# Bidirectional RWKV recurrence in a two-block kernel: running sums in two buffers, the next chunk's exponentials and keys begun mid-step, the first keys ahead of the rows, another order at the end of a step on VectorE

## The chip, the cores and the metric

The kernel runs on one core of a Trainium2 chip. The metric is device time in microseconds, the median of several runs. TensorE (PE in the profile), VectorE (DVE), ScalarE (ACT), GpSimd (POOL) and the queue of SyncE (SP) each run their own list of instructions in order and meet only through semaphores.

## The reference, cut to what matters

Two transformer blocks in fp32 follow each other. The first one mixes the tokens with a short convolution and a recurrence of RWKV type in two directions, the second one with a chunked linear recurrence and sliding window attention; each ends in a feed-forward layer. The change touches only the recurrence of the first block:

```python
def step(S, inp):                       # per token, 8 heads of 64x64 state
    r_t, w_t, kk_t, b_t, v_t, k_t = inp
    sa = einsum("bhvk,bhk->bhv", S, kk_t)
    S = S * w_t - sa[..., None] * b_t + v_t[..., None] * k_t
    return S, einsum("bhvk,bhk->bhv", S, r_t)
# decay w = exp(-DECAY_SCALE * sigmoid(...)); b = kk * a; k_d = k * (1 + (a - 1) * k_a)
# 256 context tokens, then 512 tokens of x, once forward and once in reverse; y is the sum of both
```

## The kernel before, in words

The kernel is one program of about 35,000 instructions. Most of its time goes into large fp32 products with 128x512 operands (`split_product`, L677). In between, from about 251 to 541 us of the span, stands the recurrence.

The recurrence works on chunks of L = 64 tokens: 12 chunks (NC), the first 4 (NCC) of the context and 8 (NCX) of x, in both directions d = 0 and 1, all 8 heads at once. Within a chunk the token-by-token recursion is replaced by a triangular system whose inverse is built by doubling over levels 2 to 6. The work is a software pipeline. Every engine runs `for n in range(-2, NC)`, and one step n does three things: it ends chunk n (state in, updates, results), inverts the system of chunk m = n + 1, and prepares chunk q = n + 2 (decays, keys, score products). The order within a step is written out by hand in each engine's list:

- VectorE (L2322): `running_sums(q)` (the scan over the gates, L2244) right behind the first `w_out`; then `x_out` and `x_turned` (L2257, L2264) for levels 2 to 5, `w_out` (L2250), `state_out` (L2300, L2302), the sum for `mod` (L2347). At the end of the step stand `scores_out` (L2293, one for each direction), `w_out` level 6, `first_level` (L2280), `first_turned` (L2287) and `y_last` (L2271).
- ScalarE (L1618): `update_in`, `update_out`, `state_padded`, then `decay_exps(q)` (L1587 to L1591, which exponentiates the running sums and overwrites them with the inverse decays), the copy of `ada_row2` (L1632), `tok_out` (L1597), `keys_in(q + 1)` (8 small operations, L1610), and in steps 4 to 7 `first_result` (L1603), which empties the bank of the results.
- GpSimd (L1961): the decayed rows `kt`, `rt` (L1947, 128x256), the decayed keys `bh`, `kh` (L1947, 64x256, four for each direction) and `undecayed(q + 1)` (L1956, L1957).
- TensorE (L994): `state_in`, `nx` and `dx` (both go through `tiles`, L810), `updates`, a part of another product (`ada_parts`, L623), `state_terms` (L928), `turned` (L894, which reads the key buffer `bk` and so frees it), `results` (L943, L946), and late in the step `scores(q, 0)`, `dx` level 5, `scores(q, 1)` (L883, L885), `nx` and `dx` level 6.

`scores(q, d)` waits for the keys and rows of chunk q (`kt`, `rt`, `bh`, `kh`), for the masks of the chunk before (`nk`), and (L875) for `y_out` of step n: the results bank must be empty. There is one buffer for the running sums per direction (`cum`), one `bk`, and three each of `ktrt` and `plast`.

Ahead of the loop, TensorE and VectorE turn the values (`values_turned`, `values_out`, L2218) and then form a bonus term (`bonus_sum`, `bonus_out`, L2223); GpSimd waits for all of both before it forms the first rows and keys.

Of the kernel before, what the change touches and what calls it, by code (L numbers as in the profile page):

```python
# [171 lines left out]
def two_blocks(nc, xT, ctxT, vec, con, band, w8, w11, lora, gup, outT):  # L172
    with ExitStack() as ctx:
# [144 lines left out]
        gup_sb = Area(NARENA - 4 * P).take(4 * P)  # L318
# [7 lines left out]
        class Scan:  # L326
# [9 lines left out]
            def rest(self, d):  # L336

                A = AS if d else AV
                self.ktrt = A.take(3, NJ, 2 * L)
                self.nk = A.take(2, 2, NJ, 2 * L)  # L340
                self.cum = rstd[:, NJ * L * d:NJ * L * d + NJ * L].rearrange("p (j t) -> p j t", j=NJ)
# [5 lines left out]
                self.plast = AS.take(3, NJ)  # L347
# [8 lines left out]
        assert AV.at <= 9 * TT and AS.at <= NARENA - 4 * P  # L356
# [52 lines left out]
        sem("x_in", "ctx_in", "vec_in", "con_in", "con_in2", "lora_in", "ada_in0", "ada_in1", "ada_in2", "slot_in0", "slot_in1")  # L409
# [113 lines left out]
        def _(sp):  # L523
# [57 lines left out]
            sp.dma_start(gup_sb, gup).then_inc(s["lora_in"], 16)  # L581
# [28 lines left out]
        def _(pe):  # L610
# [222 lines left out]
            def values_turned(c):  # L833

                pe.wait_ge(s["pre_out"], NJ + max(c, 0))
                for j in range(NJ):
                    at = (4 + j) * TT + L * c
                    last = nc.tensor.transpose(banks[6 + c % 2][:, P * j:P * j + P], kv_row[:, at:at + 2 * L], ident)
                last.then_inc(s["pre_mm"], 1)

            def bonus_sum(j):
                pe.wait_ge(s["pre_out"], NJ + NC + 1 + j - 1)
                mm(banks[6 + j % 2][:, :], headones, rkr[:, j, :], start=True, stop=True).then_inc(s["pre_mm"], 1)
# [3 lines left out]
            pe.wait_ge(s["lora_in"], 32)  # L847
# [8 lines left out]
            for c in range(-1, NC):  # L856
                values_turned(c)
            pe.wait_ge(s["rkr"], NJ)
            for j in range(NJ):
                bonus_sum(j)  # L860
            pe.wait_ge(s["gate"], 2 * NJ)
# [190 lines left out]
            for j in range(NJ):  # L1052
                mm(banks[j][:, :], headones, y_sum[:, j, :], start=True, stop=True).then_inc(s["y_mean"], 1)
            for j in range(NJ):
                mm(banks[4 + j][:, :], gup_sb[:, j * P:(j + 1) * P], g_lo, start=True,
                   stop=True).then_inc(s["gate_mm"], 1)
# [327 lines left out]
        def _(se):  # L1384
# [194 lines left out]
            def decay_exps(q):  # L1579

                for d, sc in enumerate(scans):
# [4 lines left out]
                    done("S", d, q - 2)  # L1586
                    act_f(sc.pe[:, :, at:at + L], sc.cum, ACT.Exp, scale=-DECAY).then_inc(s[f"pe{d}"], 1)  # L1587
                    act_f(sc.plast[:, q % 3, :], sc.cum[:, :, end], ACT.Exp, scale=-DECAY).then_inc(s[f"pe{d}"], 1)
                for d, sc in enumerate(scans):
                    done("pe", d, 2 * q + 2)  # L1590
                    act_f(sc.cum, sc.cum, ACT.Exp, scale=DECAY).then_inc(s[f"einv{d}"], 1)  # L1591
# [25 lines left out]
            keys_in(0)  # L1617
            for n in range(-2, NC):  # L1618
# [9 lines left out]
                if q < NC:  # L1628
                    decay_exps(q)
# [6 lines left out]
                if q + 1 < NC:  # L1636
                    keys_in(q + 1)
# [288 lines left out]
        def _(pool):  # L1926
# [31 lines left out]

            undecayed(0)
            pool.wait_ge(s["pre_out"], 2 * NJ + NC + 1)  # L1960
            for n in range(-2, NC - 2):  # L1961
                q = n + 2
                for d, sc in enumerate(scans):
                    at = place(d, q)
                    done("pe", d, 2 * q + 1)
                    done("gu_mm", d, 2 * (q - 3) + 1)
                    times(sc.ktrt[:, q % 3, :, 0:L], kk[:, :, at:at + L], sc.pe[:, :, d:d + L], "kt", d)
                if q >= NCC:
                    for d, sc in enumerate(scans):
                        at = place(d, q) - TC  # L1970
                        done("y_mm", d, q - 3 - NCC + 1)
                        times(sc.ktrt[:, q % 3, :, L:2 * L], rT[:, :, at:at + L], sc.pe[:, :, 1 - d:1 - d + L], "rt", d)
# [3 lines left out]
                for d, sc in enumerate(scans):  # L1976
                    done("einv", d, q + 1)
                    done("tok_mm", d, q)
                    for e, r in enumerate(HALVES):
                        done("bh", d if e else 0, 2 * q + (e or 2 * d))  # L1980
                        times(sc.bk[r, :, 1 - e, :], gates[r, d, 1, place(d, q) // L], sc.cum[r], "bh", d)
                done("bh", 1, 2 * q + 2)
                for d, sc in enumerate(scans):
                    for e, r in enumerate(HALVES):
                        done("kh", d if e else 0, 2 * q + (e or 2 * d))
                        times(sc.bk[r, :, e, :], keys_made(d, q)[r], sc.cum[r], "kh", d)
                done("kh", 1, 2 * q + 2)
# [51 lines left out]
        def _(dve):  # L2039
# [173 lines left out]
            def values_out(c):  # L2213
                dve.wait_ge(s["pre_mm"], NJ + c + 2)
# [6 lines left out]
            def bonus_out(j):  # L2221
                dve.wait_ge(s["pre_mm"], NJ + NC + 1 + j + 1)
# [14 lines left out]
            def running_sums(q, d):  # L2237

                done("bh", d, 2 * q)
                done("kh", d, 2 * q)  # L2240
                to, gate = flat(scans[d].cum), flat(gates[:, d, 0, place(d, q) // L])
# [54 lines left out]
            def state_out(n):  # L2296
                for d, sc in enumerate(scans):
# [4 lines left out]
                    V.tensor_tensor(sc.S[:, (n + 1) % 2], sc.S[:, (n + 1) % 2], spread(sc.plast[:, n % 3, :], NJ, HD),  # L2302
# [13 lines left out]
            for d in both:  # L2316
                running_sums(0, d)
            for c in range(-1, NC):
                values_out(c)
            for j in range(NJ):  # L2320
                bonus_out(j)
            for n in range(-2, NC):  # L2322
# [21 lines left out]
                if ada:  # L2344
# [518 lines left out]
```

## Time and profile before

| | |
|---|---|
| median of 3 runs | 1637.73 us (1637.27 to 1646.07) |
| the profiled execution's own time | 1632.01 us |
| its span | 1629.7 us |
| PE busy | 1499.3 us (92%) |
| DVE busy | 904.2 us (55%) |
| ACT busy | 595.8 us (37%) |
| POOL busy | 257.0 us (16%) |
| largest group, L677 hf_hi, w_up | 424.1 us |
| L810 (the small products of the recurrence) | 147.5 us, 4224 instructions |

Busy shares are averages over stages with different limits. In the stage of the large products TensorE waits for almost nothing. In the recurrence, about 18% of the span, the engines take turns, and what a change is worth there is read from the order of events within a step. Times in the views are microseconds from the start of the span.

### The profile page before, as it was taken

Reading aid. Unit: us, or ns where it says so; the run is one execution under the profiler, and the core shown is the slowest. Engines: PE = TensorE matmul, PEld = TensorE weight load, DVE = VectorE, ACT = ScalarE, POOL = GpSimd, SP = SyncE. Lnnn points to the kernel's source line nnn. Section 1 sums busy time; section 2 is a strip of 40 time slices with the busy share of each in tenths; the row PEclk is TensorE's granted clock in tenths of the full one; section 3 lists DMA queues with packets and bytes.
Section 4 is the critical chain, followed back from the end, with each engine's and each line's share of the span. In section 5 each row is a group of like instructions: output and inputs, shape, how many; then the busy total and the mean of one; then the engine's idle time right before and its main releaser. Section 6 shows DMA issues by size and latency. Waiting matters only on the chain.

```text
span 1629.7 us, 35052 instructions
## 1 busy us (share of the span) xinstructions
PE 1499.3 (92%) x14676; PEld 1239.3 (76%) x14676; DVE 904.2 (55%) x1467; ACT 595.8 (37%) x1035; POOL 257.0 (16%) x280
## 2 busy tenths in 40 slices
PE   5899996999998697999999998999879999999997
PEld 3687873888888486887787886878758788888886
DVE  1624215677677527888896224766454655655222
ACT  3422344334442324434433223536544323232221
POOL 0000003455542010111111121000001111111111
PEclk9899997999999899999999998999979999999998
DMA  8242100333300221222223222312003222222221
GB/s 346 78 150 78 52 27 1 107 107 107 94 17 4 79 73 57 86 95 103 84 96 98 97 91 76 109 54 78 27 27 103 78 103 103 81 99 97 100 95 69
DMA packets 38744, 139.64 MB, mean 86 GB/s; under 512 B 3040, under 2 KB 3552, under 8 KB 38112
## 3 DMA queue, kind: packets, MB, share of 16 engines
q1 hardware_dynamic: 38480, 135.76, 24.4%
q8 instruction: 97, 1.59, 0.4%
q10 hardware_dynamic: 144, 2.10, 0.3%
q14 instruction: 23, 0.19, 0.0%
HBM read 135.75 MB, written 2.10 MB: 85 GB/s over the span
## 4 chain that ended last, share of the span: by engine, by line
PE 62%; DVE 14%; ACT 3%; issue 3%; POOL 0%; DVEq 0%; ACTq 0%; POOLq 0%
PE bank L677 46%; PE bank L810 7%; DVE ffn_sb L2510 5%; PE bank L687 2%; DVE arena L2293 1%; DVE w_up L2123 1%; PE bank L623 1%; PE bank L1291 1%; DVE arena L2280 1%; PE bank L883 1%; ACT w_up L1409 1%; PE bank L894 1%; PE bank L928 1%; PE bank L943 1%; ACT arena L1769 1%
## 5 line engine op out<-in xcount | busy, mean ns | idle before, releaser
L677 PE MATMUL bank<-hf_hi,w_up 128*128 128x512 f32 x1376 | 424.1, 389 | 0.0
L677 PEld LDWEIGHTS bank<-hf_hi,w_up 128*128 128x128 f32 x1376 | 258.3, 188 | 53.1
L677 PE MATMUL bank<-hf_lo,w_up 128*128 128x512 f32 x688 | 269.4, 392 | 8.1 <-DVE w_up L2123 8.1
L677 PE MATMUL bank<-act_hi,w_down 128*128 128x512 f32 x704 | 216.7, 389 | 0.0
L1409 ACT ACTIVATE w_up<-ring 128x1024 fp32r<-128x1024 f32 x88 | 93.0, 1058 | 216.2 <-PE bank L677 216.2
L2123 DVE TENSOR_TENSOR w_up<-ring,w_up 128x1024 fp32r<-128x1024 f32 x88 | 108.1, 1229 | 104.4 <-ACT w_up L1409 104.3
L810 PE MATMUL bank<-arena 64*64 64x32 f32 (+1 forms) x4224 | 147.5, 221 | 16.3 <-DVE arena L2250 9.0
L677 PEld LDWEIGHTS bank<-hf_lo,w_up 128*128 128x128 f32 x688 | 129.1, 188 | 40.9 <-DVE w_up L2123 13.4
L810 PEld LDWEIGHTS bank<-arena 64*64 64x64 f32 x4224 | 137.1, 137 | 26.3 <-DVE arena L2250 10.3
L2510 DVE SCALAR_TENSOR_TENSOR ffn_sb<-ffn_sb 128x512 f32<-128x512 f32 x176 | 151.5, 861 | 5.5
L677 PEld LDWEIGHTS bank<-act_hi,w_down 128*128 128x128 f32 x704 | 132.1, 188 | 27.3
L2020 POOL TENSOR_TENSOR act_lo<-ffn_sb,act_hi 128x512 f32 x44 | 72.9, 1656 | 440.4 <-ACT act_hi L1698 426.8
L677 PE MATMUL bank<-act_lo,w_down 128*128 128x512 f32 x352 | 137.0, 389 | 1.4 <-DVE w_down L2129 1.4
L2123 DVE TENSOR_TENSOR w_in<-ring,w_in 128x1024 fp32r<-128x1024 f32 x48 | 58.5, 1223 | 137.9 <-ACT w_in L1409 137.6
L677 PE MATMUL bank<-hx_hi,w_in 128*128 128x512 f32 x384 | 120.7, 396 | 0.0
L1409 ACT ACTIVATE w_in<-ring 128x1024 fp32r<-128x1024 f32 x48 | 50.5, 1055 | 139.2 <-PE bank L677 131.4
L1426 ACT ACTIVATE w_down<-ring 128x1408 fp32r<-128x1408 f32 x32 | 44.2, 1381 | 155.6 <-PE bank L677 155.6
L2129 DVE TENSOR_TENSOR w_down<-ring,w_down 128x1408 fp32r<-128x1408 f32 x32 | 52.1, 1627 | 86.8 <-ACT w_down L1426 86.7
L677 PE MATMUL bank<-h_hi,w_in 128*128 128x512 f32 x320 | 99.9, 394 | 0.0
L677 PEld LDWEIGHTS bank<-hx_hi,w_in 128*128 128x128 f32 x384 | 73.6, 192 | 15.3
L677 PE MATMUL bank<-hx_lo,w_in 128*128 128x512 f32 x192 | 76.5, 399 | 5.4 <-ACT arena L1484 3.6
L677 PEld LDWEIGHTS bank<-act_lo,w_down 128*128 128x128 f32 x352 | 66.1, 188 | 15.6 <-DVE w_down L2129 1.8
(316 smaller groups left out, 2343.2 us busy)
## 6 DMA issues: line engine op xcount, KB each, us to landing
ring<-w SPq DMA_DIRECT2D x76, 1024.0 KB, 4.9
ring<-w SPq DMA_DIRECT2D x32, 704.0 KB, 4.0
ring<-w SPq DMA_DIRECT2D x64, 256.0 KB, 3.0
arena<-w SPq DMA_DIRECT2D x2, 3072.0 KB, 22.8
x<-xT SPq DMA_DIRECT2D x1, 2048.0 KB, 11.8
arena<-w SPq DMA_DIRECT2D x2, 1024.0 KB, 20.2
x<-xT ACTq DMA_DIRECT2D x1, 2048.0 KB, 7.7
outT<-x SPq DMA_DIRECT2D x4, 512.0 KB, 2.7
```

Source lines behind the costliest of these rows:

```text
L623: last = mm(out[32 * q:32 * q + 32, :].rearrange("r (c m) -> r c m", c=2), siluc[:, 2 * q + k, :], w[:, :, 2 * q + k, :], start=k == 0, st ...
L677: ins = mm(out, w[:, a, k, :], of_block(b, k0 + k), start=first and k == 0 and m == 0, stop=last and k == n - 1 and m == 2)
L687: ins = mm(out, w[:, a, k, :], of_block(b, k), start=k == 0 and m == 0, stop=k == KB - 1 and m == 2)
L810: last = mm(out(j, r), lhs(j, r), rhs(j, r), start=True, stop=True)
L883: mm(bank[d][e][r, at], sc.bk[r, j, e, :], sc.ktrt[r, q % 3, j, 0:n], start=True, stop=True)
L894: last = nc.tensor.transpose(bank[d][1][:, P * j:P * j + P], sc.bk[:, j].rearrange("p e t -> p (e t)"), ident)
L1409: act_f(w[:, 0], slot_view(g)[:, at:at + blocks, :], ACT.Copy).then_inc(s["w_hi"], 1)
L1426: act_f(w_down[half][:, 0], slot_view(g, HALF), ACT.Copy).then_inc(s["w_hi"], 1)
L2020: nc.gpsimd.tensor_tensor(act_lo[:, bass.ds(j, 1), :].rearrange("p a t -> p (a t)"), silu[u], act_hi[:, bass.ds(j, 1), :].rearrange("p a t ...
L2123: V.tensor_tensor(w[:, 1], slot_view(SLOT[name] + u)[:, c * KB:c * KB + KB, :], w[:, 0], ALU.subtract).then_inc(s["w_lo"], 1)
L2129: V.tensor_tensor(w[:, 1], slot_view(SLOT[name] + half, HALF), w[:, 0], ALU.subtract).then_inc(s["w_lo"], 1)
L2510: ins = V.scalar_tensor_tensor(to, pad[u][:, n // 3:n // 3 + GRID_H, n % 3:n % 3 + GRID_W], tap_w[u][:, n:n + 1], to, ALU.mult, ALU.add)
```

## The change: what it does

- The running sums get a second buffer (`cum[q % 2]`), and `plast` a fourth.
- VectorE computes `running_sums(q + 1)` behind `x_turned` level 3 and the `mod` sum of step n instead of `running_sums(q)` behind the first `w_out`. ScalarE does `decay_exps(q + 1)` between `tok_out` and `keys_in(q + 1)` instead of `decay_exps(q)` before `ada_row2`.
- GpSimd goes direction by direction: all rows of one, then of the other, then all keys of one, then of the other. For chunk 0 the keys come ahead of the rows, and begin before the values are turned.
- Ahead of the loop, the bonus comes before the values.
- End of a step on VectorE: `x_out`/`x_turned` level 5 for both directions ahead of `scores_out(q, 0)`, then `w_out` level 6, `first_level` and `first_turned` of direction 0, `scores_out(q, 1)`, `y_last`, and `first_level`, `first_turned` of direction 1.
- The weights `gup` land in another place, later, with a semaphore of their own.

```diff
@@ ScalarE
-                    done("S", d, q - 2)
-                    act_f(sc.pe[:, :, at:at + L], sc.cum, ACT.Exp, scale=-DECAY).then_inc(s[f"pe{d}"], 1)
+                    done("S", d, q - 3)
+                    act_f(sc.pe[:, :, at:at + L], sc.cum[q % 2], ACT.Exp, scale=-DECAY).then_inc(s[f"pe{d}"], 1)
...
             keys_in(0)
+            decay_exps(0)
...
-                if q < NC:
-                    decay_exps(q)
...
                 if q + 1 < NC:
+                    decay_exps(q + 1)
                     keys_in(q + 1)
                 if NCC <= n < NCC + NCX // 2:
                     for d in range(2):
                         first_result(n, d)
@@ GpSimd
             undecayed(0)
-            pool.wait_ge(s["pre_out"], 2 * NJ + NC + 1)
+            steps.last()
+            keys_decayed(0, 0)
+            pool.wait_ge(s["pre_out"], 2 * NJ)
+            keys_decayed(0, 1)
+            rows_decayed(0, 1)
+            pool.wait_ge(s["pre_mm"], 2 * NJ + NC + 1)
+            rows_decayed(0, 0)
+            undecayed(1)
+            for q in range(1, NC):
+                for d in range(2):
+                    rows_decayed(q, d)
...
+                for d in range(2):
+                    keys_decayed(q, d)
@@ VectorE
-                done("bh", d, 2 * q)
-                done("kh", d, 2 * q)
+                done("bh", d, 2 * q - 2)
+                done("kh", d, 2 * q - 2)
...
+            for j in range(NJ):
+                bonus_out(j)
             for c in range(-1, NC):
                 values_out(c)
-            for j in range(NJ):
-                bonus_out(j)
...
-                if 0 < q < NC:
-                    for d in both:
-                        running_sums(q, d)
...
+                if q + 1 < NC:
+                    for d in both:
+                        running_sums(q + 1, d)
...
+                if inv:
+                    for d in both:
+                        x_out(m, d, 5)
+                        x_turned(m, d, 5)
                 if prep:
                     scores_out(q, 0)
                 if inv:
                     for d in both:
-                        x_out(m, d, 5)
-                    for d in both:
-                        x_turned(m, d, 5)
+                        w_out(m, d, 6)
                 if prep:
+                    first_level(q, 0)
+                    first_turned(q, 0)
                     scores_out(q, 1)
                 if inv:
                     for d in both:
-                        w_out(m, d, 6)
+                        y_last(m, d)
                 if prep:
-                    for d in both:
-                        first_level(q, d)
-                    for d in both:
-                        first_turned(q, d)
-                if inv:
-                    for d in both:
-                        y_last(m, d)
+                    first_level(q, 1)
+                    first_turned(q, 1)
@@ SyncE and TensorE
-            sp.dma_start(gup_sb, gup).then_inc(s["lora_in"], 16)
...
+            sp.wait_ge(s["bh0"], 2 * NCC)
+            sp.dma_start(gup_sb, gup).then_inc(s["gup_in"], 16)
```

## Rows read from the trace of the kernel before

**Rows 1.** Timeline before the loop: start, us, engine, line, operation, count, [idle before <-releaser]

```profile
251.72 1.28 DVE L2244 TENSOR_TENSOR_SCAN rstd<-k_,arena 128x256 f32<-128x256 f32 x2 [11.56 <-ACT arena L1547]
...
253.02 2.21 DVE L2218 COPY arena<-bank 64x256 f32<-64x256 f32 x5
...
257.61 6.64 DVE L2218 COPY x<-bank 64x256 f32<-64x256 f32 x15 [0.32 <-PE bank L838]
...
267.85 0.69 DVE L2223 TENSOR_TENSOR arena<-bank,arena 128x512 f32<-128x512 f32 x1 [0.17 <-PE bank L843]
268.62 1.32 POOL L1947 TENSOR_TENSOR arena<-arena 128x256 f32<-128x256 f32 x2 [11.91 <-DVE arena L2223]
270.07 6.36 POOL L1947 TENSOR_TENSOR arena<-arena,rstd 64x256 f32<-64x256 f32 x8
...
274.98 0.37 PE L883 MATMUL bank<-arena 64*64 64x64 f32 x2 [7.17 <-POOL arena L1947]
...
276.18 0.76 DVE L2293 TENSOR_TENSOR arena<-bank,k_ 128x256 f32<-128x256 f32 x2 [7.63 <-PE bank L885]
...
278.44 2.12 DVE L2280 COPY_PREDICATED arena<-k_,arena 64x128 f32<-64x128 uint32 x4
...
282.21 0.29 DVE L2250 TENSOR_TENSOR arena<-bank,k_ 128x128 f32<-128x128 f32 x1 [0.84 <-PE bank L810]
283.06 0.29 DVE L2250 TENSOR_TENSOR arena<-bank,k_ 128x128 f32<-128x128 f32 x1 [0.56 <-PE bank L810]
```

**Rows 2.** Busy time by stretch: window, its length, busy of PE, PEld, DVE, ACT, POOL, PEclk

```profile
273.00:279.00 6.00, 2.27 (x64) 1.95 (x64) 1.97 (x6) 0.00 (x0) 5.61 (x9) 0.50 0.00 0
...
466.00:469.00 3.00, 3.00 (x67) 3.00 (x63) 1.50 (x4) 0.00 (x0) 2.84 (x5) 0.50 0.00 0
```

**Rows 3.** Chain of work in order of time: start, us, what

```profile
281.10 3.62 PE bank L810 x64
284.72 3.57 PE bank L623 x32
...
409.93 1.86 PE bank L623 x32
...
418.47 3.34 PE bank L810 x96
...
429.60 2.99 PE bank L810 x94
```

**Rows 4.** Timeline of VectorE in step 5

```profile
416.94 0.13 DVE L2347 TENSOR_TENSOR mod<-bank,v 128x8 f32<-128x8 f32 x1
...
422.82 1.29 DVE L2293 TENSOR_TENSOR arena<-bank,k_ 128x512 f32<-128x512 f32 x2 [0.67 <-PE bank L885]
424.02 0.48 DVE L2257 TENSOR_TENSOR arena<-bank,arena 128x128 f32<-128x128 f32 x2
...
426.28 0.47 DVE L2250 TENSOR_TENSOR arena<-bank,k_ 128x128 f32<-128x128 f32 x2
426.67 1.80 DVE L2280 COPY_PREDICATED arena<-k_,arena 64x128 f32<-64x128 uint32 x4
428.50 0.77 DVE L2287 STREAM_TRANSPOSE arena<-arena 128x256 f32<-128x256 f32 x2
```

**Rows 5.** Timeline of ScalarE in step 5

```profile
411.96 0.42 ACT L1587 ACTIVATE arena<-rstd 128x256 f32<-128x256 f32 x1
...
415.52 2.75 ACT L1610 ACTIVATE arena<-arena,v 128x64 f32<-128x64 f32 x8
418.17 0.72 ACT L1603 ACTIVATE arena<-bank 128x256 f32<-128x256 f32 x2
```

**Rows 6.** Timelines of GpSimd and TensorE in step 7

```profile
462.30 4.73 POOL L1947 TENSOR_TENSOR arena<-arena,rstd 64x256 f32<-64x256 f32 x6 [0.17 <-POOL arena L1947]
...
465.63 0.33 PE L883 MATMUL bank<-arena 64*64 64x128 f32 x2 [0.82 <-issue]
```

**Rows 7.** Timeline of VectorE in step 2: `state_out` of both directions

```profile
348.51 0.68 DVE L2302 TENSOR_TENSOR arena<-arena 128x256 f32<-128x256 f32 x1
...
349.56 0.42 DVE L2302 TENSOR_TENSOR arena<-arena 128x256 f32<-128x256 f32 x1
```

More of the change, by code:

```diff
@@ L317, in two_blocks @@
         rkr = Area(at_up + 16 * P).take(4, TX)
-        gup_sb = Area(NARENA - 4 * P).take(4 * P)
+        gup_sb = gates[:, 0, 1, 2:4].rearrange("p n j t -> p (n j t)")
         xa = Area(0, x[:, :, :].rearrange("p k t -> p (k t)"))
@@ L340, in rest @@
                 self.nk = A.take(2, 2, NJ, 2 * L)
-                self.cum = rstd[:, NJ * L * d:NJ * L * d + NJ * L].rearrange("p (j t) -> p j t", j=NJ)
+                self.cum = [rstd[:, NJ * L * d:NJ * L * d + NJ * L].rearrange("p (j t) -> p j t", j=NJ), AS.take(NJ, L)]
                 self.bk = AS.take(NJ, 2, L)
@@ L346, in rest @@
                 self.tok = AS.take(NJ, 2, L)
-                self.plast = AS.take(3, NJ)
+                self.plast = AS.take(4, NJ)
         scans = [Scan(), Scan()]
@@ L355, in two_blocks @@
         ada_row2 = AS.take(4, P)
-        assert AV.at <= 9 * TT and AS.at <= NARENA - 4 * P
+        assert AV.at <= 9 * TT
         A3 = Area(staged + 6144)
@@ L846, in _ @@
             pe.wait_ge(s["head_root"], 1)
-            pe.wait_ge(s["lora_in"], 32)
+            pe.wait_ge(s["lora_in"], 16)
             kk_spread(0)
@@ L855, in _ @@
                 gate_terms(NJ + i)
-            for c in range(-1, NC):
-                values_turned(c)
             pe.wait_ge(s["rkr"], NJ)
@@ L860, in _ @@
                 bonus_sum(j)
+            for c in range(-1, NC):
+                values_turned(c)
             pe.wait_ge(s["gate"], 2 * NJ)
@@ L1585, in decay_exps @@
                     done("rt", d, q - NCC)
-                    done("S", d, q - 2)
-                    act_f(sc.pe[:, :, at:at + L], sc.cum, ACT.Exp, scale=-DECAY).then_inc(s[f"pe{d}"], 1)
-                    act_f(sc.plast[:, q % 3, :], sc.cum[:, :, end], ACT.Exp, scale=-DECAY).then_inc(s[f"pe{d}"], 1)
+                    done("S", d, q - 3)
+                    act_f(sc.pe[:, :, at:at + L], sc.cum[q % 2], ACT.Exp, scale=-DECAY).then_inc(s[f"pe{d}"], 1)
+                    act_f(sc.plast[:, q % 4, :], sc.cum[q % 2][:, :, end], ACT.Exp, scale=-DECAY).then_inc(s[f"pe{d}"], 1)
                 for d, sc in enumerate(scans):
                     done("pe", d, 2 * q + 2)
-                    act_f(sc.cum, sc.cum, ACT.Exp, scale=DECAY).then_inc(s[f"einv{d}"], 1)
+                    act_f(sc.cum[q % 2], sc.cum[q % 2], ACT.Exp, scale=DECAY).then_inc(s[f"einv{d}"], 1)
             def tok_out(m, d):
@@ L1957, in undecayed, with rows_decayed @@
                     steps.do(nc.gpsimd.tensor_tensor(kd, kd, kT[:, :, at:at + L], ALU.mult))
-            undecayed(0)
-            pool.wait_ge(s["pre_out"], 2 * NJ + NC + 1)
[L1961 to L1972, printed above, removed]
+            def rows_decayed(q, d):
+                sc, at = scans[d], place(d, q)
+                done("pe", d, 2 * q + 1)
+                done("gu_mm", d, 2 * (q - 3) + 1)
+                times(sc.ktrt[:, q % 3, :, 0:L], kk[:, :, at:at + L], sc.pe[:, :, d:d + L], "kt", d)
+                if q >= NCC:
+                    at -= TC
+                    done("y_mm", d, q - 3 - NCC + 1)
+                    times(sc.ktrt[:, q % 3, :, L:2 * L], rT[:, :, at:at + L], sc.pe[:, :, 1 - d:1 - d + L], "rt", d)
@@ new lines, in keys_decayed @@
+            def keys_decayed(q, d):
+                sc = scans[d]
+                done("einv", d, q + 1)
+                done("tok_mm", d, q)
+                for e, r in enumerate(HALVES):
+                    if e:
+                        done("bh", d, 2 * q + 1)
+                    times(sc.bk[r, :, 1 - e, :], gates[r, d, 1, place(d, q) // L], sc.cum[q % 2][r], "bh", d)
+                for e, r in enumerate(HALVES):
+                    if e:
+                        done("kh", d, 2 * q + 1)
+                    else:
+                        done("bh", d, 2 * q + 2)
+                    times(sc.bk[r, :, e, :], keys_made(d, q)[r], sc.cum[q % 2][r], "kh", d)
+                done("kh", d, 2 * q + 2)
@@ L1975, in _ @@
                 done("rt", 1, q - NCC + 1)
[L1976 to L1987, printed above, removed]
+                for d in range(2):
+                    keys_decayed(q, d)
                 if q == NCC:
@@ L2237, in running_sums @@
             def running_sums(q, d):
-                done("bh", d, 2 * q)
-                done("kh", d, 2 * q)
-                to, gate = flat(scans[d].cum), flat(gates[:, d, 0, place(d, q) // L])
+                done("bh", d, 2 * q - 2)
+                done("kh", d, 2 * q - 2)
+                to, gate = flat(scans[d].cum[q % 2]), flat(gates[:, d, 0, place(d, q) // L])
                 if d == 1:
@@ L2301, in state_out @@
                     steps.last()
-                    V.tensor_tensor(sc.S[:, (n + 1) % 2], sc.S[:, (n + 1) % 2], spread(sc.plast[:, n % 3, :], NJ, HD),
+                    V.tensor_tensor(sc.S[:, (n + 1) % 2], sc.S[:, (n + 1) % 2], spread(sc.plast[:, n % 4, :], NJ, HD),
                                     ALU.mult).then_inc(s[f"S{d}"], 1)
```

11 lines of the change are left out of this document (6 added, 5 removed).

## The prediction

> **What bounds the kernel now.** I read the page first, then the chain of work in order of time, then the timelines of the single engines in a few steps. Outside the recurrence nothing is touched, so only its 290 us count. Within a step TensorE is nearly always at work: the chain of step 5 runs through L810 and L623 from nx level 2 to the 96 instructions at 418.47, which end at 421.81, and then leaves TensorE for VectorE, which is busy without a gap from 422.82 until nx level 2 of the next step at 429.60 [rows 3, 4]. So a step of 22.65 us has some 15 us bound by TensorE and 8 us in which VectorE's order decides. Three places leave an engine idle: the start, where TensorE waits 7.17 us for the first keys [rows 1]; the scores of steps 7 to 9, which wait 0.82 us (one of three such waits, 0.82 to 0.85) for GpSimd [rows 6]; and a wait of TensorE for VectorE at the end of each step.
>
> **The start.** Before, values (253.02) and bonus end at 268.54, GpSimd follows at 268.62 with 2 rows of 0.66 us and 8 keys of 0.80 us, and the scores start at 274.98, after the sixth key [rows 1]. Afterwards the same VectorE work stands in the other order: four bonus products of 0.69 us with two short waits, 253.0 to about 256.5, then about 0.8 us until the first turned values, then the values' 11.2 us (253.02 to 264.25): they end at 268.4, no gain there. But GpSimd makes its 8 keys and one row meanwhile (from about 257.7, for 7.1 us), and only one row of 0.66 us is left behind the last turned values. Scores of direction 0 start at 268.6, those of direction 1 right behind. VectorE then starts 1.2 us later (as 274.98 to 276.18), and its new order costs 0.68 + 1.06 + 0.38 + 0.68 + 1.06 + 0.40 = 4.26 us for both directions (half of each pair in rows 1, the turns by rows 4). The second nx begins at 269.8 + 4.26 = 274.1. Before, the first began at 281.10 and the second about 0.85 us later (as the two w_out, 282.21 and 283.06), 281.95 [rows 1, 3]. Gain: **7.9 us**. The scan for chunk 1 (1.28 us), now ahead of the scores' masks, lies under the 1.2 us in which TensorE forms the scores.
>
> The granted clock at this place was 0.50, the lower of the two levels, after TensorE had been idle from 267.8 [rows 2]. It made `ada_parts` 3.57 us where it is 1.86 us at full clock, and the first 64 of L810 3.62 us, about 1.1 too long [rows 3]. If the shorter idle keeps the full clock, up to 2.8 us more are saved; if not, none. I take half, **1.4 us**.
>
> **The ends of steps.** Let s be the start of scores(q, 0). Before: s = 421.65 (1.17 ahead of 422.82), second nx at 430.08, s + 8.43 [rows 3, 4]. After: dx level 5 starts at s + 0.90, VectorE's x_out 0.71 later, s + 1.61; it does nothing between. x_out and x_turned direction by direction take 1.35 us, scores_out 1.20, w_out 0.39, first_level of one direction 0.93, its turn 0.37, scores_out 1.18, y_last 0.40, first_level 0.92, turn 0.42 (pitches from one start to the next, [rows 4]). Their sum puts the second nx at s + 8.8: **+0.39 us** per step. The first nx may start a microsecond sooner, but the second and all that TensorE has queued behind it does not. dx level 6 starts sooner too, and nothing comes of it. In the narrow steps -1, 0 and 1 the same sum gives +0.22, +0.28 and +0.28, and step 2 +0.35; with step 3 that is **+1.5 us**.
>
> **A moved wait.** ScalarE's list is in order: decay_exps(q + 1), keys_in, first_result. Afterwards decay_exps waits for the scan, which VectorE starts behind `mod` at 417.0 [rows 4]. The scans' 0.67 us put the first exponential at 417.7 and the second at 418.3; the keys start at 419.45 instead of 415.52, take 2.65 us, and first_result of direction 0 (0.38 us) ends at 422.5 instead of 418.55 [rows 5]. scores(q, 0) needs y_out of this step: it starts at 422.53 instead of 421.65, and behind it on TensorE stand dx level 5 and everything VectorE needs. **+0.88 us** in steps 4, 5, 6. With the end of step, 3 x 1.27 = **+3.8 us**. Step 7 has no `ada` and ran into the GpSimd wait: 465.9 instead of 465.63, +0.28 + 0.39 = **+0.7 us**. That decay_exps leaves its old place shortens ScalarE's list there by 1.56 us (411.96 to 413.52) and brings nothing: ScalarE's copy of `ada_row2` behind it waits for TensorE's `ada_parts`, which end at 411.8 [rows 3].
>
> **GpSimd off the path.** The keys can start when `turned` frees bk, not after the rows: direction 0's are ready 2.8 us sooner. In steps 8 and 9 the wait of 0.82 to 0.85 us goes; in step 8 second_result now stands behind the scan and costs 0.17. Net with the end of step -0.28 and -0.41: **-0.7 us**. Elsewhere these keys were in time already.
>
> **The port.** In step 2 the first state product took 0.68 us while GpSimd worked, the second 0.42 us without it [rows 7]; four of first_level took 2.12 us where the first ran beside GpSimd, 1.80 us where none did [rows 1, 4]. The scans ran while GpSimd waited; they move into its busiest stretch, and in steps 0 to 3 first_level will lie beside its early rows. Bounds: 0, and 7.4 us (22 scans at 0.26 and 16 operations of first_level at 0.32 are 10.8; 13 or so of the scans, 3.4, fall in steps in which ScalarE has time). Most scans delay only ScalarE, which matters in four steps; I take **+1.5 us**.
>
> The Trainium skill (SBUF — State Buffer, section "SBUF: two separate sides") says that VectorE with two inputs in SBUF and GpSimd lock each other out of a shared port for a whole instruction. By that rule each scan would stand up to one GpSimd operation (0.72 to 0.80 us) longer; the row shows 0.26. With the full lock the steps 4 to 7 would lose up to 1.5 us each, and the sum would be near no change from before. The rule speaks against this change; the trace agrees in kind and not yet in size.
>
> **What costs nothing.** The gup load leaves the queue ahead of W_INB and goes behind the last paced load, long before it is read at 541 us. `lora_in` isn't waited for longer than the one load that stays. The wider waits on cum, S and plast are loosened by a whole step. The scan between w_out and x_out level 2 was covered by nx and dx on TensorE. If that cover were gone it would be worth 1.26 us a step; it is not.
>
> **Sum.** -7.9 - 1.4 + 1.5 + 3.8 + 0.7 - 0.7 + 1.5 = -2.5 us. The profiled execution's own 1632.0 would be 1629.5; the median of the runs is 5.7 us above it, and there I predict 1637.7 - 2.5 = **1635.2 us**. About 0.5%, 8 us, is what a measurement of this kernel can tell from no change: the forecast is no change.
>
> **Rivals.**
> 1. *The steps don't lose.* first_result is in time after all and the end of the step gains the 0.7 us in which dx level 6 waited for w_out, in 10 steps; clock full at the start. For: TensorE does wait there. Against: the second nx hangs on VectorE's sum, and the list is serial. Time: 1637.7 - 7.9 - 2.8 - 0.7 - up to 4 = about 1625 to 1627. Chance 0.14.
> 2. *The clock falls in the steps (slower).* In step 7 the clock stood at 0.50 from about 466 to 469.5 after a wait of 0.82 us [rows 2, 6], and the stretch from s to the second nx took 9.6 us instead of 8.4: 1.2 us. After the change TensorE waits about 1 us more per step, in two places within 9 us. If the clock falls in k of the 9 steps, and the port costs 4, the sum is -9.3 + 5.3 + 4 + 1.2 k: it decides from k = 1 on, and k = 7 gives 1646. Against: the other steps had waits as long without a fall. Chance 0.12, half of it beyond 8 us.
> 3. *The full port lock.* As above, +1.5 us in four steps, ScalarE later everywhere else at no cost: about 1638 to 1640. Chance 0.14.
> 4. *The start does not gain.* The bonus, now first, is held up by TensorE's own order or by a low clock, so that the values end 3 to 4 us later. Against: at 253 both sums are ready. Time: about 1639. Chance 0.08.
>
> My own forecast has 0.52. The range of 8 in 10 reaches to 1627.5 (rival 1) and to 1643. Faster by over 0.5%: 0.13; within: 0.81; slower: 0.06.
>
> **What would show it.** At the start, scores at 268 to 269 instead of 274.98 and the second nx near 274. In steps 4 to 6, the keys of L1610 starting near 419.5 by the old clock of the step, first_result ending after nx level 5, and a wait of TensorE at L883 for ScalarE of about 0.9 us; a step of about 23.9 us instead of 22.65. In steps 8 and 9 no wait for GpSimd ahead of L883. VectorE idle for about a microsecond between w_out 5 and x_out 5. If steps 4 to 6 stay at 22.65 us or less, the wait on y_out was misjudged; if the scans take over 1 us, the port was.

## The result and the profile after

The changed kernel took **1654.95 us** (median of 11 runs, 1648.13 to 1661.26) against 1637.15 us (11 runs) for the kernel before on the same chip: ratio 1.0102, 95% interval 1.0086 to 1.0118, or **+17.8 us**. The prediction was 1635.2 us in a range of 1627.5 to 1643, so the time lies outside it, on the slower side.

The profiled execution's span grew from 1629.7 to 1654.0 us, its mean clock fell from 0.964 to 0.951. Executions differ in where the recurrence begins, so times at the start are counted from the first scan: 251.72 before [rows 1], 249.52 after. From there to the first instruction behind the recurrence (before L1053 at 541.96, after L1054 at 569.18) it is 290.2 us before and 319.7 after: +29.4 us; the unchanged rest of the program differs by -5.1 us between these two executions. The profiled execution of the kernel before (1632.01 us) lies 5.1 us under its median, that of the changed kernel (1656.38) 1.4 above, so a difference read from the two views is some 6 us larger than that of the medians.

The start, by the timelines of the changed kernel (as in [rows 1]: start, us, engine, line, operation, count, [idle before <-releaser]):

```profile
249.52 1.27 DVE L2262 TENSOR_TENSOR_SCAN rstd<-k_,arena 128x256 f32<-128x256 f32 x2 [11.55 <-ACT arena L1549]
...
253.54 0.69 DVE L2241 TENSOR_TENSOR arena<-bank,arena 128x512 f32<-128x512 f32 x1 [1.57 <-PE bank L844]
...
255.01 0.69 DVE L2241 TENSOR_TENSOR arena<-bank,arena 128x512 f32<-128x512 f32 x1 [0.78 <-PE bank L844]
256.45 3.54 DVE L2236 COPY arena<-bank 64x256 f32<-64x256 f32 x8 [0.75 <-PE bank L839]
...
266.56 0.68 POOL L1949 TENSOR_TENSOR arena<-arena 128x256 f32<-128x256 f32 x1 [3.92 <-PE bank L839]
...
267.61 0.27 PE L884 MATMUL bank<-arena 64*64 64x64 f32 x2 [1.12 <-POOL arena L1949]
...
273.22 2.77 PE L811 MATMUL bank<-arena 64*64 64x32 f32 x48 [2.00 <-DVE arena L2305]
275.92 3.18 PE L624 MATMUL bank<-ring,siluc 128*32 128x256 f32 x32
```

One GpSimd row of 0.68 us is all that is left behind the last values, and the scores start 18.1 us behind the first scan instead of 23.3 [rows 1]. The second nx starts 23.7 us behind it; before it was 30.2 (281.95). That is 6.5 us gained. `ada_parts` still takes 3.18 us, near the 3.57 at the lower clock and far from the 1.86 at the full one [rows 3].

The steps, by the timelines of step 2 (353 to 361) and step 5 (430 to 440) of the changed kernel:

```profile
356.81 0.13 DVE L2362 TENSOR_TENSOR mod<-bank,v 128x8 f32<-128x8 f32 x1
356.87 1.74 DVE L2262 TENSOR_TENSOR_SCAN arena<-k_,arena 128x256 f32<-128x256 f32 x2
358.53 0.46 DVE L2268 TENSOR_TENSOR arena<-bank,k_ 128x128 f32<-128x128 f32 x2
...
358.85 2.67 PE L811 MATMUL bank<-arena 64*64 64x32 f32 x62 [1.54 <-DVE arena L2268]
...
433.15 0.13 DVE L2362 TENSOR_TENSOR mod<-bank,v 128x8 f32<-128x8 f32 x1
433.20 1.75 DVE L2262 TENSOR_TENSOR_SCAN rstd<-k_,arena 128x256 f32<-128x256 f32 x2
...
433.90 0.42 ACT L1589 ACTIVATE arena<-rstd 128x256 f32<-128x256 f32 x1 [2.05 <-DVE rstd L2262]
...
436.02 2.75 ACT L1612 ACTIVATE arena<-arena,v 128x64 f32<-128x64 f32 x8
438.67 0.63 ACT L1605 ACTIVATE arena<-bank 128x256 f32<-128x256 f32 x2
...
439.39 0.48 PE L884 MATMUL bank<-arena 64*64 64x128 f32 x2 [1.37 <-ACT arena L1605]
```

Two waits of TensorE are new. In step 2 VectorE turns from `mod` to the two scans (1.74 us) and only then forms w for level 4 (L2268), which dx level 4 reads and for which TensorE has waited 1.54 us. The same row, 1.54 or 1.55 us long, stands in each of the steps -1 to 3. In step 5 the scans hold up ScalarE: exponentials, keys, then `first_result`, and the scores wait 1.37 us for it (1.36, 1.37, 1.39 and 1.74 us in steps 4 to 7, where [rows 6] had 0.82 for GpSimd in step 7).

The groups of TensorE's waits in the changed kernel, cut to 265 to 545 us (us in total, times, longest):

```profile
PE bank L811 <- DVE arena L2268: 9.9, 9, 1.5
PE bank L811 <- DVE arena L2305: 9.6, 10, 2.0
PE bank L884 <- ACT arena L1605: 5.9, 4, 1.7
```

What the waits cost beyond their length is in the windows. First a part of step 0, then steps -1, 0, 5 and the sum of all ten steps of the changed kernel (a step runs from `turned` to `turned`; columns: length, busy us of PE, PEld, DVE, ACT, POOL with counts, PEclk, DMA share, GB/s):

```profile
306.00:309.00 3.00, 1.46 (x55) 1.33 (x45) 2.79 (x8) 1.03 (x5) 2.80 (x3) 1.00 0.56 174
309.00:312.00 3.00, 3.00 (x76) 3.00 (x74) 1.83 (x6) 3.00 (x10) 2.72 (x4) 0.54 0.29 94
...
318.00:321.00 3.00, 3.00 (x68) 3.00 (x68) 2.85 (x9) 0.38 (x1) 0.00 (x0) 0.50 0.34 108
321.00:324.00 3.00, 3.00 (x88) 3.00 (x84) 0.58 (x2) 0.77 (x3) 0.00 (x0) 0.69 0.03 5
...
280.10:303.60 23.50, 21.22 (x587) 19.67 (x585) 15.16 (x44) 8.25 (x23) 10.46 (x14) 0.85 0.29 93
303.60:328.80 25.20, 23.66 (x586) 22.29 (x584) 15.58 (x46) 8.26 (x23) 10.47 (x14) 0.73 0.29 87
...
430.10:457.10 27.00, 24.51 (x650) 22.66 (x648) 16.52 (x46) 10.45 (x29) 11.74 (x16) 0.87 0.26 81
...
sum 248.80, PE 225.19 PEld 210.59 DVE 161.85 ACT 92.86 POOL 115.65; mean PE 22.52 PEld 21.06 DVE 16.18 ACT 9.29 POOL 11.57
```

The same windows of the kernel before:

```profile
289.40:309.60 20.20, 19.05 (x586) 17.11 (x584) 14.52 (x44) 8.13 (x23) 9.89 (x14) 1.00 0.38 108
...
413.90:436.50 22.60, 21.49 (x650) 19.49 (x648) 15.68 (x46) 10.36 (x30) 11.50 (x17) 1.00 0.32 97
...
457.30:479.80 22.50, 20.78 (x589) 19.86 (x585) 15.68 (x45) 9.75 (x29) 11.18 (x16) 0.92 0.01 4
...
sum 211.70, PE 198.26 PEld 182.16 DVE 154.99 ACT 90.37 POOL 108.71; mean PE 19.83 PEld 18.22 DVE 15.50 ACT 9.04 POOL 10.87
```

TensorE idles more (248.80 - 225.19 = 23.6 us against 13.4), but the larger part of the 37.1 us by which the ten steps grew is its busy time: 26.9 us more for the same instructions, at a clock that was 1.00 in nine of ten steps before and is 1.00 in none after. The view of before flatters a little: the kernel `only the new start` below has the same loop, and in its profiled execution the ten steps took 214.8 us, three of them at 0.92 or 0.93. In step 0 of the changed kernel the clock is at its full level (2.4 GHz) through the wait of 1.54 us that ends at 308.69, then at half (1.2 GHz) for some 13.6 us of unbroken work (by PEclk, from about 309.2 to 322.9).

### The profile page after: what moved, and what is told of

Read it like the earlier page. It is cut to its first block, busy times and chain, and to the rows that moved or that the text cites. A ratio compares the mean times of both kernels' runs of the same rounds, so it can differ in the third digit from the quotient of the medians.

```text
span 1654.0 us, 35031 instructions
## 1 busy us (share of the span) xinstructions
PE 1521.2 (92%) x14676; PEld 1262.5 (76%) x14676; DVE 911.8 (55%) x1467; ACT 596.7 (36%) x1035; POOL 261.4 (16%) x280
## 4 chain that ended last, share of the span: by engine, by line
PE 73%; DVE 17%; ACT 5%; issue 3%; DMA 1%; SPq 1%; DVEq 0%; ACTq 0%
PE bank L678 54%; PE bank L811 6%; DVE ffn_sb L2527 5%; PE bank L688 2%; PE bank L884 1%; DMA arena<-w 1%; DVE w_up L2141 1%; PE bank L624 1%; DVE arena L2298 1%; DVE arena L2311 1%; DVE w_in L2141 1%; ACT w_up L1411 1%; SPq L534 1%; PE bank L895 1%; PE bank L929 1%
## 5 line engine op out<-in xcount | busy, mean ns | idle before, releaser
L811 PE MATMUL bank<-arena 64*64 64x32 f32 (+1 forms) x4224 | 163.8, 233 | 23.9 <-DVE arena L2268 10.6
L811 PEld LDWEIGHTS bank<-arena 64*64 64x64 f32 x4224 | 155.0, 151 | 32.9 <-DVE arena L2268 11.7
L678 PEld LDWEIGHTS bank<-hf_lo,w_up 128*128 128x128 f32 x688 | 129.1, 188 | 40.9 <-DVE w_up L2141 13.6
```

Of the source, the lines that this page charges most:

```text
L678: ins = mm(out, w[:, a, k, :], of_block(b, k0 + k), start=first and k == 0 and m == 0, stop=last and k == n - 1 and m == 2)
L811: last = mm(out(j, r), lhs(j, r), rhs(j, r), start=True, stop=True)
```

## The experiments

**The scan back at its old place.** In the changed kernel only the place of the scans is undone:

```
                     for d in both:
                         w_out(m, d, 2)
+                if q + 1 < NC:
+                    for d in both:
+                        running_sums(q + 1, d)
...
-                if q + 1 < NC:
-                    for d in both:
-                        running_sums(q + 1, d)
                 if inv:
                     for d in both:
                         w_out(m, d, 4)
```

> The changed kernel with one edit: VectorE computes the sums of chunk q + 1 behind the first w_out, where the kernel before had those of chunk q, instead of behind x_turned level 3. Theory A (the scans in their new place hold up w_out level 4 and, through ScalarE's list, first_result; each wait of TensorE of about 1.4 us is followed by a stretch at the lower clock): both waits go (1.54 us ahead of dx 4 in steps -1 to 3, 1.37 us ahead of scores in steps 4 to 7) and so do nearly all stretches at 0.50; steps of about 20.5 and 23 us; 1630 to 1636 us. Rival B (the new order at the end of a step is what costs): the wait for w_out 4 goes, 5 x 1.5 = 8 us less than the changed kernel, but steps stay over 23 us and the clock keeps falling: about 1645.

Measured: 1627.15 us (10 runs), ratio 0.9949 (0.9926 to 0.9971), 10.7 us faster than before and 28.5 us less, against before, than the changed kernel. The groups of VectorE's instructions by line (busy us, mean ns of one, idle before) in this kernel:

```profile
L2262 DVE TENSOR_TENSOR_SCAN rstd<-k_,arena 128x256 f32<-128x256 f32 x12 | 8.0, 707 | 11.6 <-ACT arena L1549 11.6
L2262 DVE TENSOR_TENSOR_SCAN arena<-k_,arena 128x256 f32<-128x256 f32 x12 | 7.7, 680 | 0.2 <-issue 0.2
```

and in the changed one:

```profile
L2262 DVE TENSOR_TENSOR_SCAN arena<-k_,arena 128x256 f32<-128x256 f32 x12 | 10.2, 892 | 0.0
L2262 DVE TENSOR_TENSOR_SCAN rstd<-k_,arena 128x256 f32<-128x256 f32 x12 | 10.0, 872 | 11.6 <-ACT arena L1549 11.6
```

Here `first_result` is done in time (in step 4 at 392.5 us, the scores start without a wait at 393.78), and the ten steps sum up to 217.3 us with 201.25 us of busy TensorE (changed: 248.80 and 225.19). Its recurrence, from the first scan to the first instruction behind, takes 288.8 us where the changed kernel's takes 319.7. The place of the scans is the cause of the loss. The forecast had the direction and its cause; the time came out 3 us below its range.

**Something for TensorE to do.** The changed kernel with three products per step whose results nothing reads (six records, 1.56 us at full clock), put where the new wait is:

```
+            def keep_busy(q):
+                done("nk", 0, 2 * q)
+                done("tok", 0, q)
+                for _ in range(3):
+                    mm(bank[0][1][:, 0:256], ident, k_[:, 0:2 * P], start=True, stop=True)
...
                         nx(m, d, 4)
+                    if n < NCC:
+                        keep_busy(q)
...
                 if prep:
+                    if n >= NCC:
+                        keep_busy(q)
                     scores(q, 0)
```

> The changed kernel with 3 products of 128x128 by 128x256 more in every step on TensorE, whose results nobody reads: in steps -1 to 3 between nx and dx of level 4, from step 4 on ahead of scores(q, 0), so that they fill the waits of 1.5 and 1.4 us. All waits between the engines stay. Theory A (a wait of that length is what brings the clock down): the stretches at 0.50 shrink or go and the kernel gets 8 to 14 us faster than the changed one, 1641 to 1647, though it does more. Rival (the clock falls for another reason, or costs nothing as other engines bound the step): the stretches stay, and the kernel is as slow or up to 5 us slower, 1655 to 1660.

Measured: 1644.07 us (10 runs), ratio 1.0044 (1.0018 to 1.0070): 11.6 us of the 17.8 are back, though there is more work and the scans stand where they stood. The sum of its ten steps, and the added products by line:

```profile
sum 229.90, PE 213.13 PEld 191.83 DVE 160.86 ACT 92.93 POOL 116.21; mean PE 21.31 PEld 19.18 DVE 16.09 ACT 9.29 POOL 11.62
...
L998 PE MATMUL bank<-k_ 128*128 128x256 f32 x66 | 18.5, 420 | 0.0
```

The clock is 1.00 in nine steps and 0.93 in one. Less the 16.8 us of added products (60 of the 66) TensorE is busy for 196.3 us, about as before the change (198.3). So the 37.1 us of these profiled executions split into 248.8 - 229.9 = 18.9 us that the clock cost and 18.2 us of all the rest: the waits as such, the new end of a step, and what the added products and the one step at 0.93 still cost. The Trainium skill (TensorE: Matmul & The Clock Gate, section "HAM oscillation — how this bites in real kernels") describes waits in a loop after each of which the next products run at half clock; its example has waits of 3 to 5 us, here 1.54 us were enough. It prices the penalty at half the time spent at the lower clock; that gives an estimate of about 36 us here (some 72 us at the lower clock, by PEclk of the ten windows). The runs show less, 26.9 us of busy time and 18.9 us of length. That part of a step hangs on VectorE and not on TensorE is a likely reason; no run isolates it.

**The wait alone.** The kernel before, with two scans over constants, read by nothing, ahead of w_out level 4 in steps -1 to 3:

```
+                if inv and n < NCC:
+                    for d in both:
+                        steps.do(V.tensor_tensor_scan(rstd_c[:, :], reset, reset, 0.0, ALU.mult, ALU.add))
+                        steps.last()
                 if inv:
                     for d in both:
                         w_out(m, d, 4)
```

> The kernel before with two more scans on VectorE (about 1.4 us, over constants, result unused) ahead of w_out level 4 in steps -1 to 3, where the change put its scans. Nothing else moves. If a wait of TensorE costs only its length: 5 x 1.4 = 7 us more, about 1644 to 1645, the granted clock in the steps at 1.00. Theory A (the wait is followed by a stretch at 0.50): 5 x 3.5 to 5 = 17 to 25 us more, 1655 to 1662, with stretches at 0.50 in steps -1 to 3.

Measured: 1655.77 us (4 runs), ratio 1.0130 (1.0103 to 1.0157): +19.4 us for five waits, inside the 17 to 25 expected. TensorE's timeline and windows in it:

```profile
314.64 3.06 PE L810 MATMUL bank<-arena 64*64 64x32 f32 x62 [1.76 <-DVE arena L2250]
...
315.00:318.00 3.00, 3.00 (x76) 3.00 (x77) 1.92 (x6) 0.00 (x0) 2.76 (x5) 0.54 0.28 92
318.00:321.00 3.00, 3.00 (x89) 3.00 (x84) 1.78 (x7) 0.00 (x0) 2.03 (x3) 0.50 0.45 107
...
sum 234.30, PE 215.88 PEld 201.61 DVE 163.83 ACT 90.30 POOL 111.27; mean PE 21.59 PEld 20.16 DVE 16.38 ACT 9.03 POOL 11.13
```

The waits add up to about 8.8 us (5 x 1.76); the steps grow by 22.6, of which 17.6 are busy time of TensorE. With none of the change's other parts the stretch at half clock is the same as in the changed kernel. The wait alone costs more than twice its length. Not all of that lies in the five steps: steps 4 to 6, to which nothing was added, also show 0.92 or 0.93 here, where the view of before has 1.00.

**Half the wait.** The same with one scan:

```
-                    for d in both:
+                    for d in (0,):
```

> As before_held, but one more scan (0.7 us) instead of two ahead of w_out level 4 in steps -1 to 3. If each wait costs its own length: 5 x 0.7 = 3.5 us more than before, about 1640. Theory A says that a short wait is not followed by a low clock where a long one is: about the same 3 to 4 us, far under half of the 19 us of the two scans, and the granted clock near 1.00 in most of those steps. Rival (the clock falls with any added wait): 10 us or more, 1646 and up.

Measured: 1647.33 us (6 runs), ratio 1.0057 (1.0038 to 1.0077): +9.3 us for about 5 x 0.7. **A miss** for Theory A, which expected 3 to 4 us; the rival, that the clock falls with any added wait, came close. TensorE's timeline and windows:

```profile
292.67 2.67 PE L810 MATMUL bank<-arena 64*64 64x32 f32 x62 [0.70 <-DVE arena L2250]
...
291.00:294.00 3.00, 2.30 (x74) 2.15 (x73) 2.34 (x8) 1.81 (x6) 2.75 (x4) 1.00 0.58 180
294.00:297.00 3.00, 3.00 (x80) 3.00 (x78) 1.80 (x7) 0.00 (x0) 2.76 (x5) 0.51 0.58 169
...
300.00:303.00 3.00, 3.00 (x69) 3.00 (x67) 2.35 (x7) 0.00 (x0) 0.00 (x0) 0.50 0.47 128
```

Even 0.70 us was followed by about 10 us at half clock in step -1, and the next step, with the same 0.70 us, kept 0.92. In the kernel before a wait of 1.13 us (360.34, step 2) left the clock at 1.00. In `only the new start`, whose loop is the same, waits at that place in steps 5 and 6 (0.93 and 1.13 us, at 416.97 and 440.57) were followed by a short fall, steps at 0.93 and 0.92. The length of a wait alone does not decide; what does is open.

**The ScalarE wait alone.** The changed kernel with `first_result` ahead of the exponentials and keys:

```
                 if NCC <= n < NCC + NCX // 2:
                     for d in range(2):
                         first_result(n, d)
                 if q + 1 < NC:
                     decay_exps(q + 1)
                     keys_in(q + 1)
```

> The changed kernel with ScalarE's first_result ahead of decay_exps and keys_in. Theory A: only steps 4 to 7 change; the wait of 1.37 us at the scores and the stretch at 0.50 behind it go there, steps of 27.1 us fall to about 23.3 us, 12 to 15 us less in all: about 1640. If the clock has nothing to do with that wait: 4 x 1.4 = 5.5 us less, about 1649, with the low stretches still there. Rival B: nothing, 1654.

Measured: 1657.12 us (4 runs), ratio 1.0128 (1.0089 to 1.0167). **A miss**: no gain. ScalarE's timeline in its step 5 does what was meant:

```profile
440.56 0.38 ACT L1605 ACTIVATE arena<-bank 128x256 f32<-128x256 f32 x1 [0.63 <-PE bank L947]
440.97 0.42 ACT L1589 ACTIVATE arena<-rstd 128x256 f32<-128x256 f32 x1
```

The wait of L884 for ScalarE is gone from all four steps, and steps 5 and 6 take 23.6 and 21.7 us at clock 1.00 instead of 27.0 and 25.5. But step 4 stays at 27.1 us (0.87), and steps 7 and 8 rise by 0.6 and 1.3 us with clocks of 0.87 and 0.85 (0.93 and 0.92 in the changed kernel): in step 7 the clock falls behind two waits of 0.94 and 0.72 us (at 496.74 and 498.12) that stood in the changed kernel too, 0.40 and 0.73 us long. The untouched step -1 took 25.2 us at 0.73 instead of 23.5 at 0.85. So the ten steps are only 4.8 us shorter in the profile, the whole recurrence 2.6 us (317.1 against 319.7), and the rest of the program happened to be 8.3 us longer in this execution, the slowest of the four (1662.06). Whether the edit is worth a few us is not settled; the interval of 4 runs leaves room for about 6 us.

**The parts one at a time.** The changed kernel with its old end of step; that with the scans too at their old place; the whole loop as before behind the new start; and the kernel before with only the new end. The end, old and new:

```
-old: scores_out(q, 0); x_out, x_out; x_turned, x_turned; scores_out(q, 1); w_out 6;
-     first_level x2; first_turned x2; y_last
+new: x_out, x_turned of each d; scores_out(q, 0); w_out 6; first_level, first_turned(q, 0);
+     scores_out(q, 1); y_last; first_level, first_turned(q, 1)
```

> The changed kernel with the end of a step on VectorE as before. Theory A: at most 1 to 3 us less than the changed kernel (0.4 us a step and the waits at the end), the clock still falls in steps -1 to 7: 1650 to 1655. Rival B: 15 to 20 us less, about 1635 to 1640, and no stretches at 0.50.

> The changed kernel with two edits: the scans of chunk q + 1 behind the first w_out, and the end of a step on VectorE in the order of the kernel before. Left of the change: the start, the second buffers, the earlier exponentials, GpSimd direction by direction. Theory C (with the scans out of the way the new end of a step still costs some 0.5 to 1.5 us a step and a stretch at 0.50 in three of the steps): the steps fall to at most those of before (20.0, 20.8, 22.65 us), 20 to 21 us in steps 7 to 9 as the wait for GpSimd is gone; 3 to 8 us less than scan_old_place, about 1620 to 1624. Rival D (the new end of a step is worth something once the scans are gone): 1629 to 1633, slower than scan_old_place.

> The changed kernel with its loop as before in all four engines (sums and exponentials of chunk q in their old places, GpSimd's rows of both directions ahead of the keys, old end of a step). What stays is the work ahead of the loop: bonus before values, keys of chunk 0 ahead of the rows, gup later, two buffers. Prediction's step: 7.9 us less than before, more if the clock is up: 1637.5 - 8 = 1629 to 1630. Rival (the start's gain is given back by the clock or by waits in the first steps): 1635 to 1638.

> The kernel before with the new end of a step on VectorE alone. Prediction's step: +0.4 us in each of 10 steps and nothing else, 1641 to 1642. Theory A: the pause of TensorE ahead of the second nx grows past a microsecond and the clock falls in some of the steps, each for about 2 us more: 1642 to 1655. Rival D (the new order gains): under 1637.

| kernel | median us (runs) | ratio to before, interval | difference |
|---|---|---|---|
| changed, old end | 1652.82 (4) | 1.0118 (1.0075 to 1.0161) | +15.0 |
| changed, old end and old place of scans | 1626.56 (6) | 0.9943 (0.9925 to 0.9961) | -9.8 |
| only the new start | 1629.13 (10) | 0.9964 (0.9945 to 0.9983) | -7.2 |
| only the new end | 1640.89 (10) | 1.0021 (1.0002 to 1.0040) | +4.6 |

The start gives 7.2 us. The scans' place costs 24.8 us with the old end (+15.0 against -9.8) and 28.5 with the new. The new end alone costs 4.6 us; between the pairs that differ in it alone (17.8 and 15.0, -10.7 and -9.8) the signs differ and the intervals overlap. The second kernel came out at 1626.56 us where 1620 to 1624 was expected, a small miss, and 9.8 us less than before is not clear of the 7.2 that the start alone gives: the intervals overlap.

**A version that beats both.** That second kernel, plus unread products in the idle place at the start of step -1, three ahead of the first nx and three behind it:

```
+                if n == -1:
+                    keep_busy(3)
                 if inv:
                     for d in both:
                         nx(m, d, 2)
+                        if n == -1 and d == 0:
+                            keep_busy(3)
```

> scan_end with 3 products of 128x128 by 128x256 more on TensorE ahead of the first nx of the recurrence and 3 between the first and the second, results unused, where TensorE waits about 2 us each for VectorE. Theory A: the clock stays up at the start, which gives back some of the 3.57 against 1.86 us of ada_parts and of the first nx and dx: 2 to 3 us less than scan_end, 1623 to 1625. Rival (too late or too short to matter, or the clock falls in another place): 1626 to 1628.

Measured: **1623.16 us** (5 runs, 1621.91 to 1625.75), ratio 0.9909 (0.9890 to 0.9928), 14.9 us faster than before. Its windows of the first step and of all ten, then the same of the kernel without the products:

```profile
283.00:302.90 19.90, 18.64 (x589) 17.00 (x585) 14.94 (x44) 8.02 (x23) 10.02 (x14) 1.00 0.37 110
...
sum 213.50, PE 200.27 PEld 184.56 DVE 156.11 ACT 91.12 POOL 110.33; mean PE 20.03 PEld 18.46 DVE 15.61 ACT 9.11 POOL 11.03
```

```profile
279.20:301.70 22.50, 22.50 (x590) 21.05 (x587) 14.67 (x44) 8.03 (x23) 9.87 (x14) 0.77 0.31 97
...
sum 213.00, PE 199.94 PEld 184.22 DVE 155.32 ACT 91.21 POOL 110.49; mean PE 19.99 PEld 18.42 DVE 15.53 ACT 9.12 POOL 11.05
```

The products do in step -1 what they are for: 2.6 us less, at the full clock. Up to there (from the first scan to the first `turned`) it is 29.6 us instead of 30.6. But steps 0 to 2, at 1.00 without the products, are at 0.92 with them, and the whole recurrence takes 281.5 us instead of 282.0: in the profiles next to nothing is left of the gain. Against before the medians differ by 5.1 us (-14.9 and -9.8), and the intervals overlap by a little. That the products gain in the end is likely by the medians and not shown by the profiles.

## Why the prediction was wrong

**Right: the start.** Predicted -7.9 us; the start alone gave -7.2. The second nx starts 6.5 us sooner by its distance from the first scan. The missing 1.4 us are mostly what the prediction called two short waits: VectorE's bonus waited 1.57 and 0.78 us for TensorE, so that the values ended 17.6 us behind the first scan, where 16.7 was predicted. That is the mechanism of rival 4 at about a quarter of its price. The 1.4 us of clock did not come: it is 0.50 at 273 to 276 in the changed kernel too.

**Right in size: the end of the step.** +0.39 us per step predicted, about +4 in ten; +4.6 alone (interval 0.3 to 6.5). The medians of the pairs do not tell the term apart, but the windows of single steps at clock 1.00 do: with the new end alone the steps -1, 0 and 3 to 6 are 0.3, 0.3, 0.3, 0.4, 0.5 and 0.3 us longer than before, and with the scans at their old place steps 7 and 8 take 20.9 us each with the new end and 20.5 with the old. What goes beyond it in the kernel with only the new end lies in steps in which the clock fell (step 2: 23.8 us at 0.86 instead of 20.9 at 1.00). The wait at the first_turned of direction 1 that the sum rests on is there, 0.72 us ahead of the second nx (L811 for L2305, 423.62).

**Wrong: the step "A moved wait".** It named one wait and there were two.
- *The wait that it named* was right in mechanism and small in size: in step 5 the scores wait 1.37 us, predicted 0.88. Of the half microsecond too little nearly all is the scans, 1.75 us for the pair instead of 1.26.
- *The wait that it missed* is on VectorE. In steps -1 to 3 w_out level 4 follows `mod` at once in the kernel before, and dx level 4 on TensorE needs it. The rows on which the prediction read the place are of step 5 [rows 4]. There TensorE forms `results` behind `mod`, and VectorE idles for 2.04 us ahead of w_out level 4, which covers the scans. Steps -1 to 3 have no results, so there the scans stood on the path, at a cost that the prediction put at nothing: 5 x 1.54 us of waiting, and the lower clock behind it. VectorE in the kernel before, in step 0 and in step 5:

```profile
312.69 0.13 DVE L2347 TENSOR_TENSOR mod<-bank,v 128x8 f32<-128x8 f32 x1
312.75 0.29 DVE L2250 TENSOR_TENSOR arena<-bank,k_ 128x128 f32<-128x128 f32 x1
...
419.11 0.29 DVE L2250 TENSOR_TENSOR arena<-bank,k_ 128x128 f32<-128x128 f32 x1 [2.04 <-PE bank L810]
```


**Wrong: "The port".** The term was set to +1.5 us on the ground that most scans delay only ScalarE. The scans grew from 673 to 882 ns in the mean, 24 x 0.21 = 5.0 us, and nine pairs of them were on the path. By the full lock that the Trainium skill (SBUF — State Buffer, section "SBUF: two separate sides") describes, a pair would have grown by up to 1.44 to 1.60 us (two GpSimd operations of 0.72 to 0.80); it grew by about 0.48. The size is near that of [rows 7], 0.26 us each; the failure was in what it delays.

**Wrong in weight: rival 2, the clock.** Its direction and mechanism were right, it had a chance of 0.12, and each fall was priced at 1.2 us, from one stretch in step 7 of the kernel before [rows 2, 6], where the clock of the whole step was still 0.92. The profile of the changed kernel and the filled one show 18.9 us in ten steps, some 2 us per step; the five waits in the kernel before cost (19.4 - 8.8) / 5 = 2.1 us each beyond their length. In step 0 the low stretch is 13.6 us long, and step 1 has the same clock of 0.73. The argument against it, that other steps had waits as long without a fall, was true (1.13 us in step 2) and did not carry over. Those waits stood at the end of a step, the new ones stand in its middle, and the two of step 2 (1.13 and 0.34 us) became four (1.54, 0.63, 0.54 and 0.73). That the place or the number decides is a guess; in `only the new start` two waits at the old place were followed by a fall as well.

**Right, but hidden in the changed kernel: GpSimd off the path, as far as step 8 shows it.** No wait of L884 for it is left behind the start, but in step 8 the clock, 0.92 instead of 1.00, covers any gain: 22.6 us where it was 21.3. In the kernel with the old end and the old place of the scans, where the clock stays full, step 8 takes 20.5 us:

```profile
471.70:492.20 20.50, 19.06 (x589) 18.18 (x585) 15.36 (x45) 9.22 (x26) 11.15 (x16) 1.00 0.01 4
```

That is 0.8 us less than the 21.3 of the kernel before at the same clock, about the length of the wait that went [rows 6].

The sum by what the runs show: -7.2 for the start, +24.8 to +28.5 for the place of the scans (11.6 or more of them clock), and about 0 to +4.6 for the end. With the middle values this is about +21.8, where +17.8 was measured; the parts do not add up exactly, as the places at which the clock falls are not the same in any two kernels.

## What to carry to other kernels

An instruction that is moved ahead in an in-order engine's list delays everything behind it in every phase of the loop: read the row that follows its new place in each kind of step, not in the one that shows a gap. A wait of TensorE in a dense stretch is priced with the lower clock behind it, here two to three times its length; where it can't be removed, products that nobody reads can buy part of it back. Where two edits are independent, measure them apart: with the scans left where they were the rest gains about 10 us, of which the start alone gives 7.

## What the runs showed of the hardware

- The granted clock fell to 0.50 after idle times of TensorE of 0.70 to 1.76 us in otherwise busy stretches, and stayed there for 3 to 14 us of work; a wait of 1.13 us elsewhere left it at 1.00.
- Unread products of 1.56 us per step, put where TensorE had waited, held the clock at 1.00 in nine of ten steps (0.93 in the tenth) with the scans in the same place: 11.6 us of the median.
- A scan of 128 x 256 took 673 ns in the mean where GpSimd idled and 872 to 892 ns in the changed kernel, where ten of the twelve pairs ran while GpSimd worked. Over inputs that are constants a pair took 891 ns each there as well, but a scan alone (the kernel before with one added scan) only 753 ns. So the loss per scan is not a fixed one.
